# Ten of layer 1's 22 gate-and-up couples as seven block products

## The chip, the cores and the metric

One Trainium2 chip, one core. The metric is the device time of one execution in microseconds (us). The kernel before took 1179.43 us, the median of 3 runs.

## What is computed

A trunk of two layers over 512 tokens of width 1024, all in float32. Each layer adds a mixer (two convolutions and an attention, behind one input projection) and then a SwiGLU; the change touches only the SwiGLU of the second layer, which the code calls layer 1:

```python
def swiglu(h, w_gate_up, w_down):
    g, u = jnp.split(h @ w_gate_up, 2, axis=-1)
    return (jax.nn.silu(g) * u) @ w_down

h = modulate(rms_norm(x, norm2_g[l]), sh2, sc2)      # 512 x 1024
x = x + g2[:, None, :] * swiglu(h, w_gate_up[l], w_down[l])
```

`w_gate_up` is 1024 x 5632: 2816 gate columns and 2816 up columns, which are 22 blocks of 128 of each.

## The kernel before

**Layout.** Channels stand on the 128 partitions and tokens on the free axis. `h` is 8 chunks of 128 channels x 512 tokens. To keep float32 accuracy in TensorE's fp32r products, each operand x is held as two fp32r parts, `x_hi` (rounded by a copy into an fp32r tile) and `x_lo` (x minus `x_hi`), and a product is three matmuls: hi by hi, lo by hi, hi by lo (`product`, lines 1803 to 1805).

**Units and couples.** The weights stream in as units of 128 x 1024 floats (512 KB). In the gate-and-up stage one unit holds, for one block of 128 output columns, all 8 chunks of the contraction. Unit 2f is the gate block f and unit 2f+1 the up block f; the two make a couple. A unit is 8 chunks x 3 matmuls of 128x128 by 128x512 into one PSUM bank (`unit`). The fifth to fourteenth couples of layer 1 (f = 4 to 13) are those that the change rewrites.

**The way of a unit's weights.** SyncE loads a unit into one of two slots of `raw` (even units, the gates, in slot 0, odd ones, the ups, in slot 1); the load of a unit waits until the lower half of the unit two before it has been made (`s_wlo`). ScalarE copies `raw` into `w_hi` (`split_hi`, line 680, released by the end of the unit four before, `step`), VectorE subtracts into `w_lo` (`split_lo`, line 1115). `w_hi` and `w_lo` are rings of four units.

**The way of a couple's result.** ScalarE takes silu of the gate bank (`work_a`, line 1085), VectorE multiplies by the up bank (`work_b`, line 1710), ScalarE makes `gu_hi` (line 1088) and VectorE `gu_lo` (line 1714). The down projection reads both later. The four units of two couples use banks 0 to 3.

**Order.** Each engine runs its own instruction stream in program order, held together by semaphores; the gate-and-up stage is a loop over two couples at a time on each engine. In layer 1 the first two couples stand ahead of the loop: their sums start before the norm is done, and `late_ends` (line 1717) scales them. The norm makes `h_hi` (ScalarE, line 770) and `h_lo` (VectorE, line 1199) chunk by chunk from `work_b` (line 1191). GpSimd has nothing to do in this stage: its last work is in the mixer of layer 1.

## Time and profile before

| | |
|---|---|
| median of 3 runs | 1179.43 us (1178.69 to 1180.22) |
| profiled execution | 1180.33 us, its span 1178.5 us |
| granted TensorE clock | 1.000, 2.4 GHz |
| PE, DVE, ACT, POOL busy | 99%, 62%, 44%, 11% of the span |

The span runs from the first to the last instruction. PE is the matmul engine (TensorE) and PEld its weight loads, DVE is VectorE, ACT ScalarE, POOL GpSimd and SP SyncE. A matmul's duration in the records is its latency, and consecutive matmuls overlap, so the pace of the engine is the distance between two starts.

### The profile page before, as it was taken

How to read it: one execution, taken by the hardware profiler on the slowest of the kernel's cores; microseconds unless marked ns; L12 is line 12 of the kernel's file. 1: busy time of each engine (PE TensorE's matmuls, PEld its weight loads, DVE VectorE, ACT ScalarE, POOL GpSimd, SP SyncE). 2: the span in 40 equal slices, each digit the busy share in tenths (PEclk: the TensorE clock that was granted, in tenths of full speed). 3: DMA queues.
4: the chain of work that ended last, by engine and by line, in shares of the span. 5: the costliest groups of instructions: out<-in, count | busy, mean ns of one | idle time of the engine just before them, and what ended most of it. 6: DMA issues, size and time to landing. Idle time of an engine off the chain costs nothing.

```text
span 1178.5 us, 14456 instructions
## 1 busy us (share of the span) xinstructions
PE 1165.8 (99%) x5146; PEld 930.2 (79%) x5146; DVE 726.1 (62%) x1041; ACT 523.2 (44%) x799; POOL 125.5 (11%) x208
## 2 busy tenths in 40 slices
PE   9999999999999999999999999999999999999998
PEld 6787656878888888888888877678888888888887
DVE  7988899986555433577478988857633333333331
ACT  5566788563232322322234468966432322332220
POOL 2323333111102000121000112100000000000000
PEclk9999999999999999999999999999999999999999
DMA  8779558877565223697322763422322223233332
GB/s 306 249 180 232 136 132 281 273 226 255 196 196 171 96 91 105 234 314 255 107 89 95 173 143 72 108 72 90 125 89 97 99 90 106 89 105 101 101 105 88
DMA packets 50812, 178.85 MB, mean 152 GB/s; under 512 B 5905, under 2 KB 6033, under 8 KB 50770
## 3 DMA queue, kind: packets, MB, share of 16 engines
q1 hardware_dynamic: 30386, 107.13, 27.5%
q0 software_dynamic: 20384, 71.18, 21.7%
q8 instruction: 23, 0.38, 0.1%
q14 instruction: 19, 0.16, 0.0%
HBM read 173.05 MB, written 2.10 MB: 149 GB/s over the span
## 4 chain that ended last, share of the span: by engine, by line
PE 78%; DVE 12%; ACT 4%; issue 3%; DMA 2%; POOL 0%; DVEq 0%; ACTq 0%; POOLq 0%
PE ps L1803 21%; PE ps L1805 21%; PE ps L1804 21%; DVE uc L1303 3%; PE ps L1832 3%; PE ps L1836 1%; PE ps L2075 1%; DMA tap_sum<-tap_product 1%; PE ps L1859 1%; PE ps L1851 1%; PE ps L1852 1%; DVE w_lo L1115 1%; PE ps L1927 1%; DVE neg_max L1415 1%; ACT prob L820 1%
## 5 line engine op out<-in xcount | busy, mean ns | idle before, releaser
L680 ACT ACTIVATE w_hi<-raw 128x1024 fp32r<-128x1024 f32 x196 | 207.5, 1060 | 512.1 <-PE ps L1805 453.0
L1115 DVE TENSOR_TENSOR w_lo<-raw,w_hi 128x1024 fp32r<-128x1024 f32 x164 | 201.2, 1227 | 238.6 <-ACT w_hi L680 236.4
L1803 PE MATMUL ps<-h_hi,w_hi 128*128 128x512 f32 x824 | 328.3, 398 | 0.0
L1805 PE MATMUL ps<-h_lo,w_hi 128*128 128x512 f32 x824 | 321.0, 390 | 0.0
L1804 PE MATMUL ps<-h_hi,w_lo 128*128 128x512 f32 x824 | 320.8, 389 | 0.0
L1803 PEld LDWEIGHTS ps<-h_hi,w_hi 128*128 128x128 f32 x824 | 154.7, 188 | 43.0 <-issue 12.2
L1804 PEld LDWEIGHTS ps<-h_hi,w_lo 128*128 128x128 f32 x824 | 154.8, 188 | 33.9 <-issue 2.9
L1805 PEld LDWEIGHTS ps<-h_lo,w_hi 128*128 128x128 f32 x824 | 154.7, 188 | 32.3
L1803 PE MATMUL ps<-gu_hi,w_hi 128*128 128x512 f32 x352 | 136.9, 389 | 0.0
L1804 PE MATMUL ps<-gu_hi,w_lo 128*128 128x512 f32 x352 | 136.9, 389 | 0.0
L1805 PE MATMUL ps<-gu_lo,w_hi 128*128 128x512 f32 x352 | 136.9, 389 | 0.0
L1710 DVE TENSOR_TENSOR work_b<-ps,work_a 128x512 f32<-128x512 f32 x42 | 29.0, 691 | 106.6 <-PE ps L1805 85.2
L1803 PEld LDWEIGHTS ps<-gu_hi,w_hi 128*128 128x128 f32 x352 | 66.1, 188 | 13.8
L1804 PEld LDWEIGHTS ps<-gu_hi,w_lo 128*128 128x128 f32 x352 | 66.1, 188 | 13.7
L1805 PEld LDWEIGHTS ps<-gu_lo,w_hi 128*128 128x128 f32 x352 | 66.1, 188 | 13.6
L1869 PE MATMUL ps<-w_hi,h_hi 128*128 128x512 f32 x192 | 75.4, 392 | 1.4 <-DMA w_lo<-w_stream 1.2
L1871 PE MATMUL ps<-w_hi,h_lo 128*128 128x512 f32 x192 | 74.8, 389 | 0.0
L1870 PE MATMUL ps<-w_lo,h_hi 128*128 128x512 f32 x192 | 74.7, 389 | 0.0
L1303 DVE SCALAR_TENSOR_TENSOR uc<-ua,pcol,uc 128x512 f32<-128x512 f32 x106 | 72.9, 744 | 0.0
L820 ACT ACTIVATE prob<-ps,neg_max 128x512 f32<-128x512 f32 x64 | 43.3, 683 | 17.6 <-DVE neg_max L1415 17.4
L1481 DVE SCALAR_TENSOR_TENSOR xT<-ps,mod,xT 128x512 f32<-128x512 f32 x31 | 23.2, 749 | 40.5 <-PE ps L1805 38.3
L1415 DVE TENSOR_REDUCE neg_max<-ps 128x2 f32<-128x1024 f32 x32 | 39.0, 1219 | 12.9 <-PE ps L2050 7.5
(234 smaller groups left out, 1434.7 us busy)
## 6 DMA issues: line engine op xcount, KB each, us to landing
raw<-w_stream SPq DMA_DIRECT2D x196, 512.0 KB, 3.4
w_lo<-w_stream POOLq DMA_DIRECT2D x32, 512.0 KB, 7.9
ada_ring_gu<-ada POOLq DMA_DIRECT2D x28, 512.0 KB, 4.5
ada_ring_late<-ada POOLq DMA_DIRECT2D x28, 512.0 KB, 5.1
ada_ring_first<-ada POOLq DMA_DIRECT2D x16, 512.0 KB, 5.3
ada_ring_mid_a<-ada POOLq DMA_DIRECT2D x12, 512.0 KB, 9.5
ada_ring_mid_b<-ada POOLq DMA_DIRECT2D x12, 512.0 KB, 8.1
tap_sum<-tap_product POOLq DMA_DIRECT2D x12, 256.0 KB, 7.5
```

The source lines that it names most:

```text
L680: act.activation(w_hi[:, u % RING, :], raw[:, u % RAW, :], ACT.Copy).then_inc(s_whi, 1)
L820: act.activation(prob[:, it % PROBS, comp, :], ps[:, 2 * (it % 2) + comp, :], ACT.Exp, bias=neg_max[:, it, comp:comp + 1], accum_out=row_s ...
L1115: dve.tensor_tensor(w_lo[:, u % RING, :], raw[:, u % RAW, :], w_hi[:, u % RING, :].bitcast(F32), ALU.subtract).then_inc(s_wlo, 1)
L1303: dve.scalar_tensor_tensor(uc[:, c, :], ua[:, c, j:j + T], w, uc[:, c, :], ALU.mult, ALU.add).then_inc(s_tap, 1)
L1415: dve.tensor_reduce(neg_max[:, it, :], ps[:, b:b + 2, :], AX_X, ALU.max, negate=True).then_inc(s_max, 1)
L1803: pe.matmul(dst, whi, rhs[0][:, n, :], start=start, stop=False)
L1804: pe.matmul(dst, wlo, rhs[0][:, n, :], start=False, stop=False)
L1805: return pe.matmul(dst, whi, rhs[1][:, n, :], start=False, stop=stop)
L1832: pe.matmul(ps[:, bank, :], wp[:, u % RING, n * P:(n + 1) * P], rhs[0][:, n, :], start=b == 0 and wp is w_hi, stop=False)
L1869: pe.matmul(ps[:, bank, :], hs[0], ws[0], start=n == 0, stop=False)
L1870: pe.matmul(ps[:, bank, :], hs[0], ws[1], start=False, stop=False)
L1871: return pe.matmul(ps[:, bank, :], hs[1], ws[0], start=False, stop=n == KC - 1)
```

## The change

Couples f = 4 to 13 of layer 1 are computed by Strassen's algorithm in Winograd's form, in which seven block products stand for eight. The eight blocks of a couple are: the contraction in two halves (channel chunks 0 to 3 and 4 to 7), the tokens in two halves of 256, and gate and up. A block product is 4 chunks x 3 matmuls of 128x128 by 128x256, and there are seven of them for a couple, which is 84 matmuls for 48 before.

- **Token combinations**, once: ScalarE writes `h` unsplit as well (`norm_full`), VectorE makes four combinations of its quarters, ScalarE and VectorE split each in two parts (`token_combinations`, `first_parts`).
- **Weight sums**, per couple: VectorE makes four sums of 128x512 from the couple's raw gate and up halves (`weight_sum`), and of the seven weight parts ScalarE makes seven upper halves of 128x512 (`part_hi`) and VectorE seven lower ones (`part_lo`). The rings hold eight such parts, so part k of a couple takes its slot when product k-1 of the couple before is done. SyncE's load of the next gate unit waits for lower half 3 and that of the next up unit for lower half 5.
- **Banks.** The products of a couple go to banks 4 or 5 (by turns), 6 and 7. ScalarE copies product 0 into bank 7, product 1 into `part_5` and the sum after product 2 into `part_w`; products 2, 3 and 4 wait for these copies. VectorE adds the two halves of the gate, ScalarE takes silu, VectorE multiplies in two halves.
- **gu's lower half.** ScalarE writes minus `work_b`, rounded to fp32r, into `gu_lo` (`gu_negative`), and a transfer that GpSimd issues adds `work_b` to it (256 KB a couple). `work_b` may be written again two couples later, when that transfer has landed.

The loops of the four remaining couples of layer 1 start at couple 14. Layer 0 is unchanged.

```diff
+S_FIRST, S_END = 4, 14
+S_PAIRS = S_END - S_FIRST
+S_COL = UE // 2
+S_TOK = T // 2
...
+        h_full, at = place("h_full", [P, KC, T], at=gu_lo_base + 4 * T * S_FIRST)
...
+        comb_hi, at = place("comb_hi", [P, 4, KC // 2, S_TOK], F32R, at=gu_base + 4 * T * S_END)
...
+        w_sum, at = place("weight_sums", [P, 4, S_COL], at=cb_base)
...
+        B_G, B_5, B_2 = (4, 5), 6, 7
...
+        def part_slot(w, q, k):
+            s = (7 * q + k) % (2 * RING)
+            return w[:, s // 2, s % 2 * S_COL:(s % 2 + 1) * S_COL]
+        def part_source(k):
+            gate, up = raw[:, 0], raw[:, 1]
+            return (up[:, 0:S_COL], w_sum[:, SUM_3], w_sum[:, SUM_2], gate[:, S_COL:UE], w_sum[:, SUM_1],
+                    up[:, S_COL:UE], w_sum[:, SUM_4])[k]
+        def part_done(eng, q, k):
+            if k in ALONE:
+                eng.wait_ge(s_qp, len(ALONE) * q + ALONE[k])
+            else:
+                eng.wait_ge(s_unit, U_S + 2 * q + (1 if k == 3 else 2))
...
+            for q in range(S_PAIRS):
+                f = S_FIRST + q
+                pool.wait_ge(s_gneg, q + 1)
+                pool.dma_start(gu_lo[:, f, :], wb[:, f % 2, :], accum_op=ALU.add).then_inc(s_gulo[q % 2], 16)
...
+            def norm_full(l, k):
+                a = mod_at(SH2, k)
+                act.activation(h_full[:, k, :], wb[:, k % 2, :], ACT.Identity,
+                               bias=mod[:, l, a:a + 1]).then_inc(s_hf, 1)
...
+            def part_hi(q, k):
+                u = U_S + 2 * q
+                if q and k:
+                    part_done(act, q - 1, k - 1)
+                elif q > 1:
+                    part_done(act, q - 2, 6)
+                if k in (0, 5):
+                    unit_raw_wait(act, u + 1, 0, 0)
+                elif k == 3:
+                    unit_raw_wait(act, u, 0, 0)
+                else:
+                    act.wait_ge(s_ws, 4 * q + SUM_OF[k] + 1)
+                hi = act.activation(part_slot(w_hi, q, k), part_source(k), ACT.Copy)
+                if k in OWN_LO:
+                    hi.then_inc(s_qhi, 1)
+                else:
+                    hi.then_inc(s_whi, 1)
...
+            def gu_high(l, f):
+                act.wait_ge(s_pr, FC * l + f + 1)
+                act.activation(gu_hi[:, f, :], wb[:, f % 2, :], ACT.Copy).then_inc(s_ghi, 1)
+            def gu_negative(f):
+                act.activation(gu_lo[:, f, :], wb[:, f % 2, :], ACT.Copy, scale=-1.0).then_inc(s_gneg, 1)
...
+            def first_parts(l):
+                for k in range(4):
+                    act.wait_ge(s_comb, k + 1)
+                    act.activation(comb_hi[:, k], comb[:, k], ACT.Copy).then_inc(s_chi, 1)
...
+                if q:
+                    gu_high(l, f - 1)
+                part_done(act, q, 0)
+                act.activation(ps[:, B_2, 0:S_TOK], ps[:, bank, 0:S_TOK], ACT.Copy).then_inc(s_seed, 1)
+                if q:
+                    gu_negative(f - 1)
+                if not last:
+                    part_hi(q + 1, 0)
+                part_done(act, q, 1)
+                act.activation(part_5[:], ps[:, B_5, 0:S_TOK], ACT.Copy).then_inc(s_p5, 1)
+                if not last:
+                    part_hi(q + 1, 1)
+                    part_hi(q + 1, 2)
+                part_done(act, q, 2)
+                act.activation(part_w[:], ps[:, bank, 0:S_TOK], ACT.Copy).then_inc(s_pw, 1)
...
+                else:
+                    part_hi(q + 1, 3)
+                    part_hi(q + 1, 4)
+                    part_hi(q + 1, 5)
+                act.wait_ge(s_gadd, 2 * q + 2)
+                act.activation(wa[:, f % 2, :], wa[:, f % 2, :], ACT.Silu).then_inc(s_sg, 1)
...
+                else:
+                    part_hi(q + 1, 6)
...
                 dve.scalar_tensor_tensor(wb[:, k % 2, :], xT[:, k, :], gain[:, l, which, k:k + 1],
                                          rstd[:, 0, :], ALU.mult, ALU.mult).then_inc(s_t, 1)
...
+                def weight_sum(q, i):
+                    u = U_S + 2 * q
+                    gate, up = raw[:, 0], raw[:, 1]
+                    one, two = slice(0, S_COL), slice(S_COL, UE)
+                    if i == SUM_1:
+                        unit_raw_wait(dve, u, 0, 0)
+                        x, y, op = gate[:, one], gate[:, two], ALU.add
+                    elif i == SUM_3:
+                        unit_raw_wait(dve, u + 1, 0, 0)
+                        x, y, op = gate[:, one], up[:, one], ALU.subtract
+                    elif i == SUM_2:
+                        dve.wait_ge(s_ws, 4 * q + SUM_1 + 1)
+                        x, y, op = w_sum[:, SUM_1], up[:, one], ALU.subtract
+                    else:
+                        dve.wait_ge(s_ws, 4 * q + SUM_2 + 1)
+                        x, y, op = up[:, two], w_sum[:, SUM_2], ALU.subtract
+                    dve.tensor_tensor(w_sum[:, i], x, y, op).then_inc(s_ws, 1)
...
+                def token_combinations():
+                    one, two, n = slice(0, S_TOK), slice(S_TOK, T), KC // 2
+                    a, b = h_full[:, 0:n, one], h_full[:, n:KC, one]
+                    c, d = h_full[:, 0:n, two], h_full[:, n:KC, two]
+                    dve.wait_ge(s_hf, KC)
+                    for i, (x, y) in enumerate(((c, d), (a, comb[:, COMB_Y]), (c, a), (b, comb[:, COMB_Z]))):
+                        if i == COMB_Z:
+                            dve.wait_ge(s_comb, COMB_Y + 1)
+                        elif i == COMB_V:
+                            dve.wait_ge(s_comb, COMB_Z + 1)
+                        dve.tensor_tensor(comb[:, i], x, y, ALU.subtract).then_inc(s_comb, 1)
+                    for i in range(4):
+                        dve.wait_ge(s_chi, i + 1)
+                        dve.tensor_tensor(comb_lo[:, i], comb[:, i], comb_hi[:, i].bitcast(F32),
+                                          ALU.subtract).then_inc(s_clo, 1)
...
+                def second_half_gate(q):
+                    part_done(dve, q, 4)
+                    dve.wait_ge(s_p5, q + 1)
+                    dve.tensor_tensor(wa[:, (S_FIRST + q) % 2, S_TOK:T], ps[:, B_G[q % 2], 0:S_TOK], part_5[:],
+                                      ALU.add).then_inc(s_gadd, 1)
...
+                def second_half_product(q):
+                    f = S_FIRST + q
+                    part_done(dve, q, 6)
+                    dve.tensor_tensor(wb[:, f % 2, S_TOK:T], ps[:, B_G[q % 2], 0:S_TOK], wa[:, f % 2, S_TOK:T],
+                                      ALU.mult).then_inc(s_pr, 1)
...
+                    last = q == S_PAIRS - 1
+                    if not last:
+                        weight_sum(q + 1, SUM_1)
+                    if q:
+                        second_half_product(q - 1)
...
+                        return
+                    for i in (SUM_3, SUM_2, SUM_4):
+                        weight_sum(q + 1, i)
+                    for k in range(4):
+                        part_lo(q + 1, k)
+                    first_half_gate(q)
+                    part_lo(q + 1, 4)
+                    second_half_gate(q)
+                    part_lo(q + 1, 5)
+                    first_half_product(q)
+                    part_lo(q + 1, 6)
...
                         swiglu_step(i, i == 0, M_GU + 4 * i)
                 else:
+                    begin = S_END // 2
                     late_ends()
+                    first_parts()
+                    for q in range(S_PAIRS):
+                        seven_products(q)
+                    for i in range(2):
+                        dve.wait_ge(s_gulo[i], 16 * (S_PAIRS // 2))
...
+            def seven_products(q):
+                one, two, n = slice(0, S_TOK), slice(S_TOK, T), KC // 2
+                quarter = lambda k, c: tuple(t[:, k * n:(k + 1) * n, c] for t in (h_hi, h_lo))
+                combined = lambda i: (comb_hi[:, i], comb_lo[:, i])
+                g = B_G[q % 2]
+                plan = ((g, quarter(0, one)), (B_5, combined(COMB_Y)), (g, combined(COMB_Z)), (B_5, combined(COMB_V)),
+                        (g, combined(COMB_X)), (B_2, quarter(1, one)), (g, quarter(1, two)))
+                for k, (bank, rhs) in enumerate(plan):
+                    start, stop = k in (0, 1), k in (3, 5, 6)
+                    if k in OWN_LO:
...
+                        pe.wait_ge(s_wqlo, len(OWN_LO) * q + OWN_LO[k])
+                    else:
+                        pe.wait_ge(s_wlo, lo_by_vector(U_S + 2 * q + (0 if k == 3 else 1)))
+                    if q == 0 and 1 <= k <= 4:
+                        pe.wait_ge(s_clo, {1: COMB_Y, 2: COMB_Z, 3: COMB_V, 4: COMB_X}[k] + 1)
+                    if k == 0:
+                        pe.wait_ge(s_pr, FC * (L - 1) + S_FIRST + q - 1)
+                    elif k == 1 and q:
+                        pe.wait_ge(s_gadd, 2 * q - 1)
+                    elif k == 2:
+                        pe.wait_ge(s_seed, q + 1)
+                    elif k == 3:
+                        pe.wait_ge(s_p5, q + 1)
+                    elif k == 4:
+                        pe.wait_ge(s_pw, q + 1)
+                    elif k == 6:
+                        pe.wait_ge(s_gadd, 2 * q + 2)
+                    hi, lo = part_slot(w_hi, q, k), part_slot(w_lo, q, k)
+                    for b in range(n):
+                        cols = slice(b * P, (b + 1) * P)
+                        dst = ps[:, bank, 0:S_TOK]
+                        pe.matmul(dst, hi[:, cols], rhs[0][:, b, :], start=start and b == 0, stop=False,
+                                  skip_group_check=True)
+                        pe.matmul(dst, lo[:, cols], rhs[0][:, b, :], start=False, stop=False, skip_group_check=True)
+                        mm = pe.matmul(dst, hi[:, cols], rhs[1][:, b, :], start=False, stop=stop and b == n - 1,
+                                       skip_group_check=True)
+                    mm.then_inc(s_qp if k in ALONE else s_unit, 1)
...
                     late_sums(l)
                     unit(U + U_GU + 3, 3, h, order)
-                with pe.Fori(1, N_GU // 4) as i:
+                if l:
+                    for j in range(4):
```

VectorE's program in this stage, before: the body of the loop over two couples (`w_lo` is a unit's lower half, `ff_silu` ScalarE's silu, `unit_done` TensorE's end of a unit; branch and register rows are among them).

```order
L1115 TENSOR_TENSOR w_lo<-raw,w_hi 128x1024 [waits weight_hi]
L1707 ISA
L1708 REGISTER_ALU [waits gu_ready]
L1709 REGISTER_ALU [waits unit_done]
L1710 TENSOR_TENSOR work_b<-ps,work_a 128x512 [waits ff_silu]
L1114 REGISTER_ALU
L1115 TENSOR_TENSOR w_lo<-raw,w_hi 128x1024 [waits weight_hi]
L1714 ISA [waits gu_hi_ready]
L1714 TENSOR_TENSOR gu_lo<-work_b,gu_hi 128x512
```

VectorE's program in this stage, after the change: from the weight sums of one couple to the last lower half of the same couple, beside the products of the couple ahead of it (`weight_sums` the four sums, `raw_landed0` and `raw_landed1` the loads of the gate and the up unit, `part_w` and `part_121` the copied products, `part_product` and `unit_done` the ends of block products).

```order
L1911 TENSOR_TENSOR weight_sums<-raw 128x512 [waits raw_landed0]
L1984 TENSOR_TENSOR work_b<-ps,work_a 128x256 [waits unit_done]
L1911 TENSOR_TENSOR weight_sums<-raw 128x512 [waits raw_landed1]
L1911 TENSOR_TENSOR weight_sums<-weight_sums,raw 128x512 [waits weight_sum]
L1911 TENSOR_TENSOR weight_sums<-raw,weight_sums 128x512 [waits weight_sum]
L1887 TENSOR_TENSOR w_lo<-raw,w_hi 128x512 [waits weight_part_hi]
L1887 TENSOR_TENSOR w_lo<-weight_sums,w_hi 128x512 [waits weight_part_hi] x2
L1887 TENSOR_TENSOR w_lo<-raw,w_hi 128x512 [waits weight_hi]
L1961 TENSOR_TENSOR work_a<-ps,part_w 128x256 [waits common_sum_copied,unit_done]
L1887 TENSOR_TENSOR w_lo<-weight_sums,w_hi 128x512 [waits weight_part_hi]
L1968 TENSOR_TENSOR work_a<-ps,part_121 128x256 [waits fifth_product_copied,part_product]
L1887 TENSOR_TENSOR w_lo<-raw,w_hi 128x512 [waits weight_hi]
```

Before, VectorE had two lower halves, one product and one `gu_lo` for a couple; now it has eleven operations of 128x512 and four of 128x256, and the subtraction that made `gu_lo` has left it.

ScalarE's program for one couple after the change (before it had two copies of 128x1024, one silu and one `gu_hi`).

```order
L866 ACTIVATE gu_hi<-work_b 128x512 [waits ff_product]
L895 ACTIVATE ps<-ps 128x256 [waits part_product]
L869 ACTIVATE gu_lo<-work_b 128x512
L858 ACTIVATE w_hi<-raw 128x512 [waits raw_landed1,unit_done]
L901 ACTIVATE part_121<-ps 128x256 [waits part_product]
L858 ACTIVATE w_hi<-weight_sums 128x512 [waits weight_sum,part_product] x2
L906 ACTIVATE part_w<-ps 128x256 [waits part_product]
L858 ACTIVATE w_hi<-raw 128x512 [waits raw_landed0,part_product]
L858 ACTIVATE w_hi<-weight_sums 128x512 [waits weight_sum,unit_done]
L858 ACTIVATE w_hi<-raw 128x512 [waits raw_landed1,part_product]
L916 ACTIVATE work_a<-work_a 128x512 [waits gate_half_summed]
L858 ACTIVATE w_hi<-weight_sums 128x512 [waits weight_sum,part_product]
```

The copies that products 2, 3 and 4 wait for stand in one line with the upper halves of the next couple, and the first row, `gu_hi` of the couple before, waits for VectorE's product.

## Rows read from the trace of the kernel before

**Rows 1.** The page: busy time of each engine.

```profile
PE 1165.8 (99%) x5146; PEld 930.2 (79%) x5146; DVE 726.1 (62%) x1041; ACT 523.2 (44%) x799; POOL 125.5 (11%) x208
```

**Rows 2.** The chain that ended last, 860 to 960 us, by line.

```profile
by line: PE ps L1803 33.6%; PE ps L1804 33.5%; PE ps L1805 33.4%
```

**Rows 3.** Busy time by stretch (stretch: us, each engine's busy time, clock, DMA share, GB/s).

```profile
865.00:974.00 109.00, 109.00 (x482) 90.28 (x482) 37.43 (x40) 31.29 (x40) 0.00 (x0) 1.00 0.29 96
```

**Rows 4.** Groups of instructions, 865 to 974 us (busy us, mean ns of one, idle before).

```profile
L1804 PEld LDWEIGHTS ps<-h_hi,w_lo 128*128 128x128 f32 x161 | 30.2, 188 | 6.3
L1115 DVE TENSOR_TENSOR w_lo<-raw,w_hi 128x1024 fp32r<-128x1024 f32 x20 | 24.5, 1226 | 40.1 <-ACT w_hi L680 40.1
L1088 ACT ACTIVATE gu_hi<-work_b 128x512 f32 x10 | 6.2, 617 | 0.0
```

**Rows 5.** Timeline of PE, 900 us (start us, us, what).

```profile
900.41 0.39 PE L1803 MATMUL ps<-h_hi,w_hi 128*128 128x512 f32 x1
...
901.09 0.39 PE L1803 MATMUL ps<-h_hi,w_hi 128*128 128x512 f32 x1
```

**Rows 6.** Timeline of PE, 15.5 us: short matmuls, each with its weight load.

```profile
15.52 2.62 PE L1810 MATMUL ps<-ones 128*128 128x128 f32 x22
```

**Rows 7.** The same matmuls by line (ns min/median/max, first and last start).

```profile
L1810 PE MATMUL ps<-ones x56: 273/421/582, 1.1 to 17.9; 128*128 128x128 f32 x56
```

**Rows 8.** Timeline of PE, 239.4 us: matmuls of 256 columns in plain f32.

```profile
239.57 1.13 PE L1885 MATMUL ps<-sq_sum,ones 128*128 128x256 f32 x4 [0.62 <-DVE sq_sum L1475]
```

**Rows 9.** Timeline of DVE, 76 us and 832 to 846 us.

```profile
76.48 0.75 DVE L1390 TENSOR_TENSOR tb<-tn,tabs 128x256 f32<-128x256 f32 x2
...
832.93 0.69 DVE L1722 TENSOR_TENSOR work_a<-ps,rstd 128x512 f32<-128x512 f32 x1
833.54 0.68 DVE L1722 TENSOR_TENSOR work_b<-ps,rstd 128x512 f32<-128x512 f32 x1
...
836.32 1.22 DVE L1115 TENSOR_TENSOR w_lo<-raw,w_hi 128x1024 fp32r<-128x1024 f32 x1
837.46 0.68 DVE L1740 TENSOR_TENSOR gu_lo<-work_b,gu_hi 128x512 fp32r<-128x512 f32 x1
...
844.55 0.68 DVE L1740 TENSOR_TENSOR gu_lo<-work_b,gu_hi 128x512 fp32r<-128x512 f32 x1
```

**Rows 10.** Timeline of ACT, 66.9 us and 97 us.

```profile
66.94 1.07 ACT L790 ACTIVATE work_a<-ps 128x512 f32<-128x512 f32 x2
...
97.34 1.05 ACT L680 ACTIVATE w_hi<-raw 128x1024 fp32r<-128x1024 f32 x1
98.30 1.04 ACT L675 ACTIVATE w_lo<-raw 128x1024 fp32r<-128x1024 f32 x1
```

**Rows 11.** Issues of transfers, 865 to 974 us (KB each, median us to landing).

```profile
raw<-w_stream SPq DMA_DIRECT2D x20, 512.0 KB, 3.3
```

**Rows 12.** Issues of transfers, 60 to 130 us, where adding transfers run.

```profile
raw<-w_stream SPq DMA_DIRECT2D x11, 512.0 KB, 6.7
tap_sum<-tap_product POOLq DMA_DIRECT2D x12, 256.0 KB, 7.5
```

**Rows 13.** Timeline of SP (the loads of `raw`) and ACT, 836 to 843 us.

```profile
836.03 0.33 SPq L531 DMA_DIRECT2D raw<-w_stream  x1
837.72 0.33 SPq L531 DMA_DIRECT2D raw<-w_stream  x1
...
839.39 1.06 ACT L680 ACTIVATE w_hi<-raw 128x1024 fp32r<-128x1024 f32 x1 [2.32 <-DMA raw<-w_stream]
...
842.32 1.06 ACT L680 ACTIVATE w_hi<-raw 128x1024 fp32r<-128x1024 f32 x1 [1.38 <-DMA raw<-w_stream]
```

**Rows 14.** The norm of layer 1: timeline of ACT, 831 us, and of PE, 827 us.

```profile
831.38 0.73 ACT L770 ACTIVATE h_hi<-work_b,mod 128x512 fp32r<-128x512 f32 x1 [0.72 <-DVE work_b L1191]
...
826.97 0.39 PE L1832 MATMUL ps<-h_hi,w_hi 128*128 128x512 f32 x1
```

More of the change, by code:

```diff
@@ L56 @@
 LATE_SUMS = 3
+S_FIRST, S_END = 4, 14
+S_PAIRS = S_END - S_FIRST
+S_COL = UE // 2
+S_TOK = T // 2
+COMB_Y, COMB_Z, COMB_X, COMB_V = range(4)
+SUM_1, SUM_3, SUM_2, SUM_4 = range(4)
+SUM_OF = {1: SUM_3, 2: SUM_2, 4: SUM_1, 6: SUM_4}
+ALONE = {0: 1, 1: 2, 2: 3, 4: 4, 5: 5}
+OWN_LO = {0: 1, 1: 2, 2: 3, 4: 4, 6: 5}
 UNITS = U_DOWN + N_DOWN
@@ L476, in encoder_kernel @@
         s_gu = sem("gu_ready")
+        s_hf = sem("h_full_ready")
+        s_comb = sem("token_combination")
+        s_chi = sem("token_combination_hi")
+        s_clo = sem("token_combination_lo")
+        s_ws = sem("weight_sum")
+        s_qhi = sem("weight_part_hi")
+        s_wqlo = sem("weight_part_lo")
+        s_qp = sem("part_product")
+        s_seed = sem("first_product_copied")
+        s_p5 = sem("fifth_product_copied")
+        s_pw = sem("common_sum_copied")
+        s_gadd = sem("gate_half_summed")
+        s_gneg = sem("gu_negated")
+        s_gulo = [sem(f"gu_lo_added{i}") for i in range(2)]
         s_store = sem("stored")
@@ L1050, in _ @@
                     norm_hi(l, 1, 0)
+                    norm_full(l, 0)
                 else:
@@ L1058, in _ @@
                     norm_hi(l, 1, k)
+                    if late:
+                        norm_full(l, k)
                     if l == 0 and k == KC - 1:
@@ L1079, in _ @@
                         act.activation(gu_hi[:, f, :], wb[:, f, :], ACT.Copy).then_inc(s_ghi, 1)
-                with act.Fori(1, N_GU // 4) as i:
+                if late:
+                    first_parts(l)
+                    for q in range(S_PAIRS):
+                        seven_products(l, q)
+                with act.Fori(S_END // 2 if late else 1, N_GU // 4) as i:
                     for j in range(4):
@@ L1190, in norm_apply @@
                     dve.wait_ge(s_h, KC * n + k - 1)
+                    if l and which:
+                        dve.wait_ge(s_hf, k - 1)
                 dve.scalar_tensor_tensor(wb[:, k % 2, :], xT[:, k, :], gain[:, l, which, k:k + 1],
@@ new lines, in gu_low, with first_parts @@
+                def gu_low(f):
+                    dve.wait_ge(s_ghi, FC * l + f + 1)
+                    dve.tensor_tensor(gu_lo[:, f, :], wb[:, f % 2, :], gu_hi[:, f, :].bitcast(F32),
+                                      ALU.subtract).then_inc(s_gu, 1)
+                def first_parts():
+                    token_combinations()
+                    for i in (SUM_1, SUM_3, SUM_2, SUM_4):
+                        weight_sum(0, i)
+                    part_lo(0, 0)
+                    part_lo(0, 1)
+                    for j in (1, 3):
+                        f = S_FIRST - 2 + j // 2
+                        dve.wait_ge(s_unit, U_S - 4 + j + 1)
+                        dve.wait_ge(s_sg, FC * l + f + 1)
+                        dve.tensor_tensor(wb[:, f % 2, :], ps[:, j, :], wa[:, f % 2, :], ALU.mult).then_inc(s_pr, 1)
+                        if j == 1:
+                            part_lo(0, 2)
+                            part_lo(0, 3)
+                            gu_low(f)
+                            part_lo(0, 4)
+                            part_lo(0, 5)
+                        else:
+                            part_lo(0, 6)
+                            gu_low(f)
@@ L2163, in _ @@
                     unit(U + U_GU + 3, 3, h, order)
-                with pe.Fori(1, N_GU // 4) as i:
+                if l:
+                    for j in range(4):
+                        pe.wait_ge(s_pr if j % 2 else s_sg, FC * l + j // 2 + 1)
+                        unit(U + U_GU + 4 + j, j, h, order)
+                    for q in range(S_PAIRS):
+                        seven_products(q)
+                with pe.Fori(S_END // 2 if l else 1, N_GU // 4) as i:
                     for j in range(4):
```

79 lines of the change are left out of this document (77 added, 2 removed).

## The prediction, on record before the run

> **What bounds the kernel now.** I read first the page's busy times: PE is busy for 99% of the span, DVE for 62%, ACT for 44% [rows 1]. The chain of waits through the changed couples shows the three matmul lines of a unit and nothing else [rows 2], and in the stretch that holds ten couples PE is busy throughout, DVE for 37 and ACT for 31 of 109 us [rows 3]. So only TensorE's own pace counts here, and the other engines have room. The reader is to see next what that pace is. Three matmuls start in 901.09 - 900.41 = 0.68 us, one in 0.227, though each record shows 0.39 [rows 5]: records overlap. A couple is 48 of them, 10.88 us, ten are 108.8. The weight load of each, shown with 188 ns, hides [rows 4].
>
> **TensorE's share of the change.** 48 matmuls of 512 columns become 84 of 256: 7/8 of the columns, and 36 weight loads more. No row shows fp32r with 256 columns. 512 columns at 2.4 GHz are 0.213 us, the row has 0.227, 0.0135 more. If the excess goes with the columns, a short one takes 0.113; if it is a cost of each matmul, 0.120. The floor is how closely loads can follow each other: 22 matmuls of 128 columns, each with a 128x128 load of its own, take 2.62 us, the last of them 0.27, so (2.62 - 0.27)/21 = 0.112 [rows 6, 7]. A couple then takes 84 of these, 9.4 (floor), 9.5 or 10.1 us of TensorE. Plain f32 of 256 columns took (1.13 - 0.38)/3 = 0.25, where 0.38 is my estimate of the last record [rows 8]; that end would be 21 us a couple. Three fp32r matmuls of twice the columns fit in 0.68, so I leave it out of the range and take 0.113 to 0.120.
>
> The Trainium skill has a rule that speaks against the change ("TensorE: Matmul & The Clock Gate", Part 3): a weight load overlaps running matmuls only where their row groups differ. All matmuls here use all 128 rows, and the trace disagrees: a load of 188 ns fits into a pace of 0.227. By the rule it would be in the open, which is the third rival below.
>
> **VectorE's and ScalarE's work.** Back to back, records overlap by 0.08 us: a 128x512 tensor_tensor is followed after 0.61 us, one of 1024 after 1.14, and two of 256 last 0.75 together, so are 0.34 apart [rows 9]. For a couple VectorE has 11 x 0.605 + 4 x 0.34 = 8.0 us, where it had 37.4/10 = 3.7. On ScalarE a copy of 1024 is followed after 0.96 (0.09 of overlap), PSUM copies of 512 after about 0.48 [rows 10]; a 512 copy shown with 617 ns [rows 4] is then 0.52 in a row, and I estimate 0.28 for 256. Ten of 0.52 and three of 0.28 are 6.0 us. Neither fills 9.5 us, but both run in order and wait for each other, so the loops of waits decide.
>
> **The loop that I expect to bind.** `raw` holds one couple. The up unit's slot is free after lower half 5, and before the next couple's lower half 5 VectorE does, in order: weight sums 3, 2 and 4 (4 waits for 2, just ahead of it: +0.17), lower halves 0 to 3, a half gate, lower half 4, the other half gate, lower half 5. That is 9 x 0.605 + 2 x 0.34 + 0.17, and 0.08 for the end of the last, 6.4 us. Ahead of it stands the load, 3.3 us from issue to landing in this stretch [rows 11], and two hand-overs, 0.18 from VectorE's end to the issue and 0.08 from the landing to its start. Together 9.9 us: longer than TensorE at 0.113 (9.5), shorter than at 0.120 (10.1). So TensorE waits a little, or just not. The gate unit's loop (load, sum 1, a half product, three sums, four lower halves) is 3.6 + 0.34 + 8 x 0.605 + 0.25 = 9.0, with 0.9 to spare.
>
> And the load need not take 3.3. Before, loads are 5 us apart. Now the up load is issued 1.9 us behind the gate's (two lower halves, two half gates). The nearest case: issues at 836.03 and 837.72, and ScalarE, which waits for the landings, starts at 839.39 and 842.32; the first took 3.3, the second 4.5 at most [rows 13]. From 865 on the median is 3.3 [rows 11]. I take 3.4 for a distance of 1.9, nearer the many than the one, and 10.0 us for a couple.
>
> **The copies between products.** Product 2 waits for ScalarE's copy of product 0. The copy stands behind `gu_hi`, which waits for VectorE's second half product, which stands behind a weight sum. From the end of product 6: 0.25 + 0.6 + 0.34 + 0.1 + 0.52 + 0.28 + 0.1 = 2.2 us, against 2.7 for products 0 and 1. It fits by 0.5, and is late as soon as the gate's load is. Product 6 waits for the second half gate, the last in VectorE's queue: there TensorE waits for what its pace leaves of the loop, 0.1 to 0.4 us.
>
> **The start.** Here cover is short. The chunk-wise units begin at 826.97 [rows 14] and are 48 matmuls, to 837.9; four ordinary units follow, to 859.6. VectorE comes free after `gu_lo` at 845.2 [rows 9], and the norm pushes that: ScalarE's eight unsplit chunks fill its gaps of 0.72, but the last delays all behind it by 0.7 [rows 14], so 845.9. In order it has 8 combinations (9.1 us), four sums (2.6), two lower halves (1.2), the product of couple 2 (0.6, to 859.6), four more lower halves and a `gu_lo` (3.1, to 862.7), the product of couple 3 (to 863.3). Then ScalarE's `gu_hi` and the copy of product 0, to 864.3. TensorE wants it at 859.7 + 2.7 = 862.4 and waits 1.9. Lower half 5 was late too (862.7), so the next up load lands at 866.2, and ScalarE's first upper half from it stands ahead of the copy of product 1: product 3 waits another 1.4. Product 6 waits 0.6. The first couple takes 9.9 + 3.9 = 13.8 us.
>
> **What costs nothing.** gu's ten transfers: 7.5 us where such ran [rows 12], wanted 15 us after issue, by the next product into the same `work_b`. The end: VectorE waits some 9 us for the last of them, under 22 us of ordinary units whose lower halves are made; without that cover it would cost those 9. The norm's chunks are wanted 3 us or more after they are ready.
>
> **The sum.** 13.8 + 9 x 10.0 = 103.8 against 108.8: 5.0 us less. The profiled execution took 1180.3 (span 1178.5), so 1175.3; the median of the runs is 0.9 below it: 1174.4, say 1174.5.
>
> **The rivals.**
> *Loads get in each other's way.* The ten couples break even at (108.8 - 13.8)/9 = 10.56 us, a load of about 4.0. With 4.5 as in [rows 13] a couple takes 11.1 and the whole 4.9 more: 1184, slower. With 6.7, as where GpSimd's adding transfers ran densely [rows 12], 13.3 and 25 more: 1204. For it speaks the one pair, and gu's new transfers; against it that a load busies the engines for about 2 us and the next comes 1.9 later, and that gu's 256 KB are issued some 4 us ahead of the gate's load.
> *Short operations cost their full records.* 0.68 and 0.42: the loop is 9.9 + 9 x 0.08 + 0.16 = 10.8, 2.2 us slower in all, 1181.6. The 0.61 of [rows 9] speaks against it.
> *The weight load shows.* 0.113 + 0.112 = 0.225 and 18.9 us a couple: 80 us slower, 1260. The 0.112 of [rows 6], load and matmul together, speaks against it.
> *Everything fits better.* TensorE at 0.113, hand-overs shorter, 9.6 a couple, the start 13.3: 9.1 us less, 1170.3.
>
> **How the numbers follow.** About 0.2% (2.4 us) is also what a measurement of this kernel can tell from no change. Forecast (1171.5 to 1177): 0.50. Better fit: 0.16. Loads of about 4, or other waits that eat the gain, 1177 to 1182: 0.16. Slower: loads near 4.5 or above 0.11, full records or a longer start 0.05, the load in the open 0.02. So faster 0.66, same 0.16, slower 0.18. The range 1169.5 to 1181.5 leaves out the slow loads and a tail of the best.
>
> **What would show it.** Matmuls of 256 columns 0.113 to 0.120 apart; a first couple of 13 to 14 us with TensorE waiting at products 2 and 3 for ScalarE's copies; then a couple every 9.8 to 10.2, TensorE's waits at product 6; VectorE waiting for the up unit's landing before its second weight sum, about 0.9 us. Wrong would be: up loads of 4 us or more, a pace above 0.13, waits at the copies in every couple, or a late norm.

## The result: 0.3% slower, outside the range

| | before | after |
|---|---|---|
| median of the runs, us | 1179.43 (1178.23 to 1180.22, 11 runs) | 1182.95 (1180.43 to 1184.95, 11 runs) |
| profiled execution, span, us | 1180.3, 1178.5 | 1182.16, 1180.4 |

The ratio is 1.0029, 95% interval 1.0022 to 1.0037. The forecast was 1174.5, range 1169.5 to 1181.5; what happened is the first rival, loads in each other's way. The profiled execution of after lies 0.8 us under the median of its runs, so what it shows is a little less than what a typical run lost.

The profile's page of after has the first line that answers to [rows 1], and the stretches that answer to [rows 3] show where the time is (busy us of each engine, granted clock, DMA share, GB/s):

```profile
PE 1161.5 (98%) x5506; PEld 942.8 (80%) x5506; DVE 782.2 (66%) x1159; ACT 567.5 (48%) x901; POOL 134.6 (11%) x218
```

```profile
859.00:869.00 10.00, 5.99 (x45) 5.68 (x46) 7.75 (x14) 5.86 (x13) 0.00 (x0) 0.98 0.32 105
869.00:872.00 3.00, 3.00 (x16) 3.00 (x16) 3.00 (x6) 1.16 (x3) 0.00 (x0) 0.50 0.03 5
872.00:876.00 4.00, 4.00 (x35) 4.00 (x35) 3.13 (x7) 1.78 (x3) 0.00 (x0) 0.99 0.65 210
```

In the first ten microseconds of the first couple TensorE has matmuls for six, and then three microseconds at a granted clock of 0.50. From 972 us on it is busy throughout, as before. So all the difference is in the ten couples. Their matmuls start 0.120 us apart in the median:

```profile
925.75 0.28 PE L2160 MATMUL ps<-h_hi,w_hi 128*128 128x256 f32 x1
925.87 0.28 PE L2162 MATMUL ps<-h_hi,w_lo 128*128 128x256 f32 x1
925.99 0.28 PE L2163 MATMUL ps<-h_lo,w_hi 128*128 128x256 f32 x1
```

84 of them are 10.08 us. The starts of the couples' first matmuls, read from the timeline of PE, give the time of each couple: 15.93, 10.08, 10.08, 10.08, 10.23, 11.28, 10.75, 10.78, 11.79 and, for the tenth, 10.08. Together 111.1 us, where before had 108.8. The waits of the stretch from 855 to 972 us (us in total, times, longest us), TensorE's own first:

```profile
PE ps L2160 <- ACT part L901: 4.0, 3, 2.4
PE ps L2160 <- ACT ps L895: 1.4, 1, 1.4
PE ps L2160 <- DVE work_a L1968: 0.8, 4, 0.2
...
DVE weight_sums L1911 <- DMA raw<-w_stream: 17.2, 13, 2.8
...
ACT w_hi L858 <- DMA raw<-w_stream: 6.4, 6, 3.2
```

TensorE waits for ScalarE's two copies (L901 of product 1, L895 of product 0) and for a half gate (L1968); behind these stand VectorE and ScalarE, which wait for the loads of `raw`. How long the loads take, from the list of instructions on `raw` between 877 and 962 us:

```profile
DMA to landing us min/median/max: 3.1/3.3/5.3
```

The median is that of before [rows 11]; the 5.3 is new. Two up loads show the pattern, one in a couple of 10.08 us, one in the couple of 11.79. First the issue, in the timeline of SP (the gate's load went out at 881.89 and at 945.74), then the load's time in the list of issues (KB each, us to landing):

```profile
884.01 0.33 SPq L593 DMA_DIRECT2D raw<-w_stream  x1
...
947.49 0.33 SPq L593 DMA_DIRECT2D raw<-w_stream  x1
```

```profile
raw<-w_stream SPq DMA_DIRECT2D x1, 512.0 KB, 3.2
...
raw<-w_stream SPq DMA_DIRECT2D x1, 512.0 KB, 5.3
```

Issued 2.12 us behind the gate's load, the first took 3.25. Issued 1.76 behind, the second took 5.28. From couple to couple the up loads took:

| up load, issued behind the gate's by | 1.70 | 2.51 | 2.12 | 2.09 | 1.99 | 1.76 | 1.76 | 1.76 | 1.76 | 1.76 |
|---|---|---|---|---|---|---|---|---|---|---|
| took, us | 4.51 | 3.21 | 3.25 | 3.36 | 4.02 | 4.77 | 4.25 | 4.29 | 5.28 | 3.95 |

The first nine belong to the second to tenth couple; the last is that of the first ordinary couple behind them, and no product of the ten waits for it.

The gate's loads, some 8 us or more behind the one ahead of them, took 3.1 to 3.3 without exception. The next rows are VectorE's, in the couple of 10.75 us, whose load took 4.25:

```profile
927.54 0.69 DVE L1911 TENSOR_TENSOR weight_sums<-raw 128x512 f32<-128x512 f32 x1 [0.44 <-DMA raw<-w_stream]
928.15 0.42 DVE L1984 TENSOR_TENSOR work_b<-ps,work_a 128x256 f32<-128x256 f32 x1
930.23 0.69 DVE L1911 TENSOR_TENSOR weight_sums<-raw 128x512 f32<-128x512 f32 x1 [1.67 <-DMA raw<-w_stream]
...
934.58 0.42 DVE L1961 TENSOR_TENSOR work_a<-ps,part_w 128x256 f32<-128x256 f32 x1
934.91 0.68 DVE L1887 TENSOR_TENSOR w_lo<-weight_sums,w_hi 128x512 fp32r<-128x512 f32 x1
935.51 0.42 DVE L1968 TENSOR_TENSOR work_a<-ps,part 128x256 f32<-128x256 f32 x1
935.85 0.68 DVE L1887 TENSOR_TENSOR w_lo<-raw,w_hi 128x512 fp32r<-128x512 f32 x1
```

After the landing (1.67 us of wait, to 930.23) VectorE has no gap up to lower half 5 at 935.85. This keeps it going: a late load makes VectorE late; being late, it no longer waits for TensorE's products 3 and 4 at the half gates; so lower half 5 follows lower half 3 without a gap, and the two loads go out 1.76 us apart instead of 2.1; and so the next up load is slow again. Where load and period stand side by side they fit: 11.28 - 4.77, 10.75 - 4.25, 10.78 - 4.29 and 11.79 - 5.28 all leave 6.5.

### The profile page after: what moved, and what is told of

It reads as the page before. It is cut to its first block and busy times, and to the rows that moved or that the text cites. A ratio compares the mean times of both kernels' runs of the same rounds, so it can differ in the third digit from the quotient of the medians.

```text
span 1180.4 us, 15383 instructions
## 1 busy us (share of the span) xinstructions
PE 1161.5 (98%) x5506; PEld 942.8 (80%) x5506; DVE 782.2 (66%) x1159; ACT 567.5 (48%) x901; POOL 134.6 (11%) x218
## 5 line engine op out<-in xcount | busy, mean ns | idle before, releaser
L746 ACT ACTIVATE w_hi<-raw 128x1024 fp32r<-128x1024 f32 x176 | 186.3, 1059 | 425.1 <-PE ps L2110 360.7
L1275 DVE TENSOR_TENSOR w_lo<-raw,w_hi 128x1024 fp32r<-128x1024 f32 x144 | 177.0, 1229 | 202.2 <-ACT w_hi L746 194.0
L2108 PE MATMUL ps<-h_hi,w_hi 128*128 128x512 f32 x664 | 266.1, 401 | 0.0
L2110 PE MATMUL ps<-h_lo,w_hi 128*128 128x512 f32 x664 | 258.7, 390 | 0.0
L2109 PE MATMUL ps<-h_hi,w_lo 128*128 128x512 f32 x664 | 258.6, 389 | 0.0
L2108 PEld LDWEIGHTS ps<-h_hi,w_hi 128*128 128x128 f32 x664 | 124.7, 188 | 36.7 <-issue 12.2
L2109 PEld LDWEIGHTS ps<-h_hi,w_lo 128*128 128x128 f32 x664 | 124.7, 188 | 27.5 <-issue 2.9
L2110 PEld LDWEIGHTS ps<-h_lo,w_hi 128*128 128x128 f32 x664 | 124.6, 188 | 26.3
L2109 PEld LDWEIGHTS ps<-gu_hi,w_lo 128*128 128x128 f32 x352 | 66.1, 188 | 13.8
L1872 DVE TENSOR_TENSOR work_b<-ps,work_a 128x512 f32<-128x512 f32 x30 | 20.7, 691 | 68.4 <-PE ps L2110 46.9
L2160 PE MATMUL ps<-comb_hi,w_hi 128*128 128x256 f32 x160 | 46.4, 290 | 5.6 <-ACT part L901 4.0
```

Source lines behind the costliest of these rows:

```text
L746: act.activation(w_hi[:, u % RING, :], raw[:, u % RAW, :], ACT.Copy).then_inc(s_whi, 1)
L1275: dve.tensor_tensor(w_lo[:, u % RING, :], raw[:, u % RAW, :], w_hi[:, u % RING, :].bitcast(F32), ALU.subtract).then_inc(s_wlo, 1)
L2108: pe.matmul(dst, whi, rhs[0][:, n, :], start=start, stop=False)
L2109: pe.matmul(dst, wlo, rhs[0][:, n, :], start=False, stop=False)
L2110: return pe.matmul(dst, whi, rhs[1][:, n, :], start=False, stop=stop)
L2160: pe.matmul(dst, hi[:, cols], rhs[0][:, b, :], start=start and b == 0, stop=False, skip_group_check=True)
```

## The experiments

Theory A: an up load issued less than some 2 us behind the gate's takes 4 us or more, and the loop of the up slot makes that the couple's time. Theory B: the loads only lie beside what binds, which is the work and hand-overs of VectorE and ScalarE. A third suspect was gu's new adding transfers; in the expectation of e1 "Theory B" stands for that suspect, in e4's for other causes in the couple, the short matmuls' traffic among them.

All ratios are to before, with 95% intervals. Couples are the periods of the profiled execution.

**Without the adding transfers** (e1_no_add; gu's lower half lacks its second term):

```diff
-                pool.wait_ge(s_gneg, q + 1)
-                pool.dma_start(gu_lo[:, f, :], wb[:, f % 2, :], accum_op=ALU.add).then_inc(s_gulo[q % 2], 16)
```

> The changed kernel without GpSimd's ten adding transfers (gu's lower half of couples 4 to 13 is left as the negative upper part, so the output is not the reference's); the waits for them become waits for ScalarE's negative copy. In the changed kernel the up unit's load took 4.0 to 5.3 us in the late couples, and a couple 10.8 to 11.8 instead of 10.08. Theory A (two loads less than 2 us apart slow the second): nothing changes, up loads issued 1.76 us behind the gate's still take 4.0 us or more, 1182 to 1184 us. Theory B (gu's adding transfers slow the loads): up loads at 3.3 us everywhere, every couple after the first at 10.08, 1179 us or less.

Measured: 1183.72 (1182.4 to 1184.63), ratio 1.0037 (1.0023 to 1.0051). First couple 15.7, then 10.08, 10.66, 10.53, 10.64, 10.51, 10.89, 11.36, 11.63; the eight up loads issued less than 1.9 us behind a gate's took 4.0 to 5.1. The transfers do not cause the slow loads. The trace of after agrees: the packets of the adding transfers (queue `software_dynamic`) run for some 1.5 us each in the gaps between loads, 879.4 to 880.9 us the first, and beside no load of the ten couples. In e1 it was an up load issued 1.96 behind the gate's that took 4.44 and was followed by the first slow couple.

**Copy of product 1 ahead of the next upper half** (e2_copy_first):

```diff
-                if not last:
-                    part_hi(q + 1, 0)
                 part_done(act, q, 1)
                 act.activation(part_5[:], ps[:, B_5, 0:S_TOK], ACT.Copy).then_inc(s_p5, 1)
                 if not last:
+                    part_hi(q + 1, 0)
                     part_hi(q + 1, 1)
```

> Only ScalarE's order is changed: the upper half 0 of the next couple, which waits for the up load, stands behind the copy of product 1 instead of ahead of it. TensorE's waits ahead of product 3 (0.3 to 1.3 us in late couples, 2.6 in the first) were for that copy. Theory A: in the first couple the 2.6 us and the stretch at half clock behind them (some 1.6 us) shrink; in later couples the wait moves to product 6, since VectorE waits for the same load, and the couples stay at 10.8 to 11.8: some 2 us less, about 1181. Rival C (only the order on ScalarE costs, VectorE would keep up): all later couples at 10.1 to 10.3 and no half clock, 1176 us.

Measured: 1184.39 (1183.28 to 1185.42), ratio 1.0046 (1.0032 to 1.006). The wait at product 3 is gone, one of 2.5 us stands at product 4, the granted clock stays at 1.00 and the first couple takes 14.9. But the up loads are 1.76 us behind the gate's from the second couple on, took 3.84 to 5.61, and the couples 10.4 to 12.1. Cured at one wait, the time came back at the next ones: neither Theory A's 1181 nor the rival's 1176 was met.

**Gate's second lower half first** (e3_gate_first), which moves the loads apart:

```diff
-                    for k in range(4):
+                    for k in (0, 3, 1, 2):
                         part_lo(q + 1, k)
```

> Only VectorE's order is changed: lower half 3 of the next couple, which frees the gate unit's slot, is made before lower halves 1 and 2, so the gate's load is issued some 1.2 us earlier and the up unit's load stands 2.9 us behind it instead of 1.76. The up load's own issue doesn't move. Theory A: up loads at 3.2 to 3.5 us, couples at 10.08 to 10.2 all the way, the first couple as before at 15.9: 1180.43 to 1178.5 us and a narrow spread. Theory B or any other cause in the couple: up loads stay at 4 us and more in late couples, 1183 us.

Measured: 1179.09 (1178.51 to 1182.95), ratio 1.0001 (0.9992 to 1.001). The up load ahead of the second couple is still issued 1.69 us behind the gate's and took 4.59, the next one 3.40 behind and 3.15; all later ones are issued 2.96 behind and took 3.19 to 3.38, one 3.86; couples 10.27, one 10.67. The times to landing, between 872 and 960 us:

```profile
DMA to landing us min/median/max: 3.1/3.3/3.9
```

Only the order of four operations on VectorE differs from after; the slow loads are gone and 3.9 us with them. What is left is the first couple, 16.0, and 0.19 in each later one.

**Before, with its loads in pairs** (e4_before_pairs): the kernel before, where TensorE has spare time to hide a load; only the waits of SP differ, so that two loads go out 0.55 us apart.

```diff
-                    sp.wait_ge(s_wlo, RAW * i + (j - RAW + 1 + made))
+                    sp.wait_ge(s_wlo, RAW * i + made)
```

> The kernel before, with the loads of its last loop (layer 1 from the first gate-and-up couples on) issued in pairs: the load of an even unit waits until the lower half of the unit just before it is made, so both loads are issued some 0.4 us apart; the ring holds four units, so TensorE shouldn't notice. It measures what closeness alone does, with no short matmuls and no adding transfers. Theory A: the first of a pair takes 3.3 us, the second 4 us or more. Theory B, or the short matmuls' traffic as the cause: both take 3.3 to 3.6.

Measured once: 1187.34. Between 861 and 1160 us the first of a pair took 3.1 to 3.4, all 28 second ones 3.8 to 5.0, median 4.0. TensorE is busy throughout from 855 to 1178 us, so what is lost lies ahead of that (the pairs begin at 832 us), 5.0 us of it in one wait at the sum of squares of the norm:

```profile
PE ps L1894 <- DVE sq_sum L1475: 5.0, 1, 5.0
```

No seven products, no adding transfers, less than half of VectorE's work in this stretch: closeness alone makes the second load slow. It also makes it no slower at 0.55 us than at 1.76.

**A second slot for the up unit** (e5_up_slot): the up load leaves the loop. The slot lies in `rstd`, free in this stretch; couple q + 1's up load is issued a couple earlier, behind the gate's load of couple q.

```diff
+        rstd_base = top[0]
         rstd = sb("rstd", [P, 2, T])
+        raw_up, _ = place("raw_up", [P, UE], at=rstd_base)
...
+        def up_slot(q):
+            return raw_up[:] if q % 2 else raw[:, 1]
...
+            for q in range(1, S_PAIRS + 1):
+                u = U_S + 2 * q
+                sp.wait_ge(s_wlo, lo_by_vector(u - 2))
+                sp.dma_start(raw[:, 0, :], w_in[u]).then_inc(s_raw[0], 16)
+                if q < S_PAIRS:
+                    sp.wait_ge(s_wlo, lo_by_vector(u - 1))
+                    load_up(q + 1)
```

> The up unit gets a second slot, so that its load is issued a couple ahead, still 1.8 us or less behind a gate's. Theory A (a load issued close behind another takes 4 to 5 us, and this one stands in the up unit's loop): loads may stay slow, but nobody waits for them. Couples 10.08 us throughout; in the first couple only the wait of 1.6 us for the seed copy at product 2 and some 0.5 at product 6, no wait of 2.6 at product 3, and with it no stretch at half clock: 12.2 us. Sum 102.9 for ten couples where before has 108.8 and after 111.1: 1173.5 to 1175. Theory B (the short operations and hand-overs of VectorE and ScalarE are the bound, the loads only lie beside them): couples stay at 10.6 to 11.8 and the time at 1180 to 1183.

Measured: 1174.87 (1173.98 to 1175.45), ratio 0.996 (0.9946 to 0.9973). Nine couples of 10.08, the first 12.7 (the expectation of e9 below takes it as 12.44, which leaves out TensorE's restart after each wait); ten are 103.4 us. TensorE's waits from 855 to 965 us are those of the first couple alone:

```profile
PE ps L2184 <- ACT ps L919: 1.4, 1, 1.4
PE ps L2184 <- DVE work_b L1970: 0.3, 1, 0.3
PE ps L2184 <- DVE work_a L1992: 0.3, 1, 0.3
PE ps L2184 <- ACT part_w L930: 0.2, 1, 0.2
```

One up load still took 5.72 us (issued at 870.31, 1.87 behind a gate's), and nobody waited for it. Theory B is out: VectorE and ScalarE do the same work here, and TensorE's pace binds. There is no stretch at half clock.

**Another order at the start** (e6_start: on the order of e3): ScalarE makes gu's upper halves of couples 2 and 3 of its ordinary units ahead of the last weight halves, VectorE the gate's lower half first and both products ahead of lower halves 4 to 6.

ScalarE's part of the edit:

```diff
...
+                act.activation(wa[:, (f + 1) % 2, :], ps[:, 2, :], ACT.Silu).then_inc(s_sg, 1)
+                gu_high(l, f)
+                part_hi(0, 4)
+                gu_high(l, f + 1)
+                part_hi(0, 5)
...
```

> The order of lower halves that set the spacing of the loads to 2.9 us (gate's second half first), and at the start of the ten couples an order in which ScalarE makes the upper halves of couples 2 and 3 of gu before the remaining weight halves, and VectorE the gate's lower half first. Theory A with the start's waits: the waits of 1.6 and 2.6 us fall to about 0.5 each and the half clock goes, first couple 11.5 instead of 16, later couples 10.27: about 4 us less than the run with only the order changed, 1175. If the start's waits come instead from work that VectorE must do there whatever its order (35 operations in 22 us), they move to product 6 or into couple two and the time stays near 1179.

Measured: 1179.62 (1178.8 to 1180.85), ratio 0.9997 (0.9988 to 1.0006): no gain. The wait at product 2 falls from 1.6 to 0.84 us and the clock stays up, but product 3 waits 2.95 and product 6 0.7. Lower half 5, ahead of the next up load, is later in this order (the load goes out at 864.0), and the copy of product 1 behind that load is late by as much. The first of the two expectations was wrong; the second had the time, but the wait went to product 3 as well.

**All four together** (e7_both; the edits are those shown).

> All four together: gate's second half first, copy of product 1 ahead of the next upper half, second slot for up, the other order at the start. Theory A: couples 10.08 from the second on, first couple 11 to 11.5, ten couples 101.7 to 102.2, clock near 1.0 throughout: 1172 to 1173.5, faster than both kernels. Theory B: no better than 1179, as with the order of lower halves alone.

Measured: 1180.09 (1179.03 to 1181.4), ratio 1.0004 (0.9995 to 1.0013), a plain miss. Couples of 10.67, each alike, with 0.52 us of wait at product 6 and no wait for a load.

**The same without the start** (e8_no_start).

> As the run with all four, but the start as in the changed kernel. Its difference to that run is the price of the start's order: first couple 12.2 with the 1.6 us at product 2, against 11 to 11.5, so 0.7 to 1.2 us slower than it: 1173.5 to 1174.5.

Measured: 1179.32 (1178.41 to 1180.59), ratio 0.9995 (0.9986 to 1.0004). Couples of 10.67 again, so the start is not the reason, and the expected 1173.5 to 1174.5 was missed as well. The waits of e8 between 875 and 960 us have VectorE waiting for ScalarE twice in each of eight couples:

```profile
DVE w_lo L1910 <- ACT w_hi L882: 16.3, 16, 1.1
```

**Second slot and the start** (e9_slot_start) and **second slot and e3's order** (e10_slot_order), to find which edit does it.

> Second slot for the up unit, and at the start the other order of ScalarE and VectorE (gu's halves of couples 2 and 3 ahead of the last weight halves), nothing else. With only the slot the first couple took 12.44 us, with waits of 1.60 at product 2, 0.32 at product 4 and 0.46 at product 6. If ScalarE's copy of product 0 is late because of VectorE's product of couple 3 alone, the wait at product 2 falls to the 0.84 seen with this order before; products 4 and 6 may wait up to 0.3 more each, so 11.7 to 12.2 us and 1174.2 to 1174.9. If VectorE's work at the start is the limit whatever its order, the waits only move and it is as with the slot alone, 1174.9.

Measured: 1174.65 (1173.45 to 1175.83), ratio 0.9957 (0.9943 to 0.9971), the same as e5. Product 2 waits 0.84 instead of 1.60, product 4 1.13 instead of 0.32: the wait moved. First couple 12.8, the others 10.08.

> Second slot for the up unit, and the gate's second lower half moved ahead of lower halves 1 and 2. The run that had these two and the copy of product 1 ahead of the next upper half took 10.67 us a couple, with 0.52 of wait at product 6 in each and no load waited for. If the moved copy makes that loop (the upper half 0 is late behind it, and lower half 0 and all behind it on VectorE), couples are 10.08 here and the time is about 1175. If the moved lower half makes it, couples stay near 10.6 and the time near 1179.

Measured: 1175.83 (1175.17 to 1177.19), ratio 0.9972 (0.9962 to 0.9983). Couples of 10.27. VectorE in it:

```profile
884.96 0.69 DVE L1911 TENSOR_TENSOR w_lo<-raw_up,w_hi 128x512 fp32r<-128x512 f32 x1
887.18 0.69 DVE L1911 TENSOR_TENSOR w_lo<-raw,w_hi 128x512 fp32r<-128x512 f32 x1 [1.52 <-ACT w_hi L882]
```

Lower half 3 (887.18) now stands second, but ScalarE makes upper half 3 only after its copy of product 2, so VectorE stands idle for 1.52 us and the half gates at the end of its queue come 0.13 us too late for product 6 (a start there 0.25 behind the last instead of 0.12), with what the restart costs 0.19 a couple. So both edits have a price where no load is in the way: the order 0.19, the copy ahead of upper half 0 another 10.67 - 10.27 = 0.40, because upper half 0, and behind it all of VectorE's lower halves, is later (in e8 ScalarE's copy of product 1 waits 0.40 us for TensorE, and VectorE 0.89 for the upper half behind it). Couples of 10.27 are what neither of the two expectations had. In e3 the order's price was paid for by loads 1 us faster.

The version with the second slot alone (or with the start's order, no difference beyond the intervals) beats both kernels: 0.4% faster than before, 0.7% than after.

## Why the prediction was wrong

**The pace: right, at the upper end.** 0.120 us, that is 84 x 0.120 = 10.08. With 512 columns it is 0.227 and with 256 0.120; columns at 2.4 GHz are 0.213 and 0.107, so what is left over is 0.013 both times, as a cost of each matmul would have it. The Trainium skill ("TensorE: Matmul & The Clock Gate", Part 1) also has the excess over N / 2.4 GHz as a fixed cost of each matmul, but gives it as 2.5 ns, where these rows have 13. The third rival, the weight load in the open, did not come, nor did the second: a half gate is followed after 0.33 us (934.58 to 934.91), not after its full 0.42.

**The loop: right in mechanism and, without the load, in size.** The prediction had 9.9 - 3.3 = 6.6 us beside the load. Measured 6.5, in four couples: with a load of 3.3 that is 9.8 against TensorE's 10.08, so the loop had 0.3 us to spare.

**The load: the step that failed.** It is this sentence: "I take 3.4 for a distance of 1.9, nearer the many than the one." The many were loads 5 us apart, and said nothing of a close pair. The one pair in the trace, 1.69 us apart [rows 13], said 4.5, and the bound from it was in the prediction as 1184 with a chance of 0.11. It was the better row: 24 up loads at 1.70 to 1.76 us in after, e1 and e2 took 3.8 to 5.6, median 4.1 to 4.4 in each run. The four slow couples come to 11.15 on average, where that rival had 11.1. Also the distance was taken as a number, 1.9, while it is a result of what binds: 2.1 as long as TensorE binds, and 1.76 as soon as VectorE does. The prediction's break-even of 10.56 a couple, a load of about 4.0, was of the right size (with the first couple as measured it is 108.8 - 15.9 over 9, 10.3, a load of 3.8).

**The first couple: mis-sized, 15.9 for 13.8.** The wait at product 2 was put at 1.9 and was 1.6. The one at product 3 was put at 1.4 and was 2.6: the chain was as told (lower half 5 late, the up load behind it, ScalarE's upper half of it ahead of the copy of product 1), but that load too was issued 1.70 us behind the gate's and took 4.51 instead of 3.3. And no step had the clock: after waits of 1.6 and 2.6 us within six, some 16 of TensorE's matmuls start 0.213 apart, 16 x 0.093 = 1.5 us. That is the lower of its two levels, 1.2 GHz. The Trainium skill (same page, Part 1) has a gate that halves the clock after idle time; in this the trace agrees with it, and has it after two waits of which the longer is 2.6. In e2, with waits of 1.6 and 2.5 and twice as many matmuls between them, and in e5, with the wait at product 3 gone, the granted clock stays at 1.00. Product 6 was put at 0.6 and did not wait; that product 3's wait and the slow stretch took its place is likely, not shown.

**Forecast and outcome, by terms.** 111.1 - 103.8 = 7.3 us in ten couples: 2.1 in the first; nine at 10.08 instead of 10.0, 0.7; and 0.15 + 1.20 + 0.67 + 0.70 + 1.71 = 4.4 for slow loads. This is the profiled execution, 1182.16 where the forecast had 1175.3. That is 6.9 apart, the medians are 8.5 apart: the runs of after spread from 1180.4 to 1185.0, and no trace of a slower one was taken that would show where the remaining 1.6 lies.

**What was put at nothing: right.** gu's transfers landed after 3.3 us in the median and e1 gained nothing without them. After 972 us TensorE is busy throughout, so the end costs nothing. Nor is the norm ahead late: in the first 855 us TensorE is busy for 845.9, before for 845.5.

**What stays open.** Why a load close behind another takes 0.5 to 2.3 us longer was not found; in e4 it is no worse at 0.55 than at 1.76. The traces narrow it in two ways.

First, slow and fast are told apart less by the distance than by how much of the load ahead is still to come. This is a count over the loads of all the traces, before's too, from 857 to 972 us (in before and e4 to 1160), without those beside which packets of another queue run. The 53 that were issued 1.2 us or more before the load ahead had landed took 3.6 to 5.0. The 53 that were issued later than that, but still ahead of its landing, took 3.1 to 3.8. In after the line lies between 1.18 us to come (the load at 2.12, which took 3.25) and 1.24 (the load at 1.99, which took 4.02).

Second, the largest values have company. The profile also lists packets of a kind `instruction`, mostly of 16 KB, and those of that size take 0.9 to 2.2 us here. The queues' view of after from 947.4 to 952.8 us, beside the load of 5.28, shows one, and so does that of e5 from 897.6 to 902.1, beside a gate load that was issued 7.5 us behind the last one and took 4.31:

```profile
q8 instruction: 1, 0.02, 1.5%
...
q8 instruction: 1, 0.02, 1.8%
```

The load of 4.77 has such packets beside it too, the other slow up loads in the table have none. In the kernels with the change all eight loads of more than 4.7 us have one, among them the 5.72 of e5, and so has e5's other slow gate load (4.43). Part of the 1.20 and 1.71 above may be theirs. No run took them away, so this is a coincidence in time and not a cause shown: four up loads of e1 and e2, 1.75 us behind the gate's, had such a packet and took 4.0 to 4.1, two up loads of e5 with one took 3.5 and 3.6, and in e4 second loads took up to 5.0 without one.

That the order of the start can be bettered is likely (2.4 us of waits remain in e5's first couple), but both tries only moved them.

## What to carry over

Measure a load's time to landing at the distance at which the change will issue it; rows of loads far apart don't bound it, and here the one close pair said more than twenty of them. In a loop where the load's slot is freed by the engine that waits for the load, the distance is itself a result: look what it becomes once the loop is late, since a loop with 0.3 us to spare can fall into a slower rhythm and stay there. And an order that pays while a load binds costs where it does not (the order of e3 gained 3.9 us with one slot and lost 1 with two): take the edit that removes the load from the loop first, and try the orders on that.

## What the chip showed that was not expected

- Two loads of 512 KB on one queue: 3.1 to 3.4 us for the first, and for the second 3.8 to 5.0 at a distance of 0.55 (28 loads), 3.8 to 5.6 at 1.70 to 1.76 (24), 3.25 to 4.44 at 1.96 to 2.12 (four in after and e1), 3.2 to 3.9 at 2.96 (eight in e3). At 2.35 to 2.62 (e5, to 962 us) six took 3.3 to 3.6; the two behind a gate load that was itself slow took 4.3 and 4.4.
- One execution goes from one pace into another: four couples of 10.1 to 10.2 us, then four of 10.8 to 11.8, tipped over by one load of 4.02 us, and no way back before the last, behind which no block product's weights are loaded.
- fp32r matmuls of 256 columns, each with a weight load of 128x128 shown with 0.19 us, start 0.120 apart for 88 us on end (e5), load and all.
